# The beginning of feed-forward 1: 23 products of the tile of ones ahead of it, the third lower part ahead of the squares' sums, the fifth and sixth lower parts within the gating chain

## The chip, the cores and the metric

The kernel runs on one core of one Trainium2 chip. The metric is the device time of one launch in microseconds (us), the median of a few runs. The engines of the core that matter here are PE (matrix products), DVE (element-wise work), ACT (activations and copies), POOL (GpSimd) and SP, whose queue issues the loads of the weights. Each engine takes its instructions in the order in which they are written; engines wait for each other through semaphores.

## The reference

The program is a transformer block (a feed-forward network, a mixer of two attentions, a second feed-forward network) followed by a second, larger block, on 256 tokens of width 1024. The change touches only the beginning of the first feed-forward network:

```
def rms_norm(x, g):
    xf = x.astype(jnp.float32)
    y = xf * lax.rsqrt(jnp.mean(xf * xf, axis=-1, keepdims=True) + EPS)
    return (y * g.astype(jnp.float32)).astype(x.dtype)

def swiglu(x, w_gate, w_up, w_down):
    return (jax.nn.silu(x @ w_gate) * (x @ w_up)) @ w_down

f1 = swiglu(rms_norm(h, ffn1_pre_g[l]), ffn1_w_gate[l], ffn1_w_up[l], ffn1_w_down[l])
h = h + 0.5 * rms_norm(f1, ffn1_post_g[l])
```

The hidden width of this network is 2816, which is 22 chunks of 128 (FC = 22).

## The kernel before

The weights come as a stream of tiles of 128 by 1024 fp32 numbers (512 KB), in the order in which PE uses them, through a ring of six places (RING = 6). Feed-forward 1 uses 66 tiles: gate 0, up 0, gate 1, up 1, down 0, gate 2, up 2, down 1, and so on. Below, "tile 0" to "tile 5" are the first six of them. SP loads the place of a tile again when PE has counted up "tiles_used" for it.

Every product is made from two parts of each number. ACT copies a tile to a rounded upper part (`upper`), DVE subtracts that from the tile for the lower part (`lower`, an instruction of 128 by 1024; POOL does it for every third tile from tile 8 on), and PE makes three matmuls in place of one (`split_product`: upper by upper, upper by lower, lower by upper, lines 641 to 643). The input and the hidden chunks are split in the same way: `input_upper` and `lower_input` for the eight chunks of the input, `upper_hidden` and `lower_hidden` for a hidden chunk. One tile is 24 matmuls of 128x256.

The norm is applied late: the gate and up products are made from the input times its gain, without the inverse root. Meanwhile ACT squares the input in four pairs (`square_pair`), DVE adds the squares (`input_sums`, four additions), PE sums over the partitions (`add_squares`), ACT takes the root (`take_root`), DVE inverts it (`invert`), PE spreads the inverse over the partitions (`spread`), and ACT copies it to memory (`copy_inverse`). Only then can DVE scale the first gate product by it, ACT apply Silu, DVE multiply with the up product, ACT and DVE split the hidden chunk, and PE begin with `down(0, 4)`, the product of hidden chunk 0 with tile 4. This row of steps is called the gating chain below. Before it PE can do four tiles (`gate_up(0, 0)` is tiles 0 and 1, `gate_up(1, 2)` is tiles 2 and 3); `add_squares` and `spread` stand between products of the latter.

After the beginning a loop of nine turns runs over the rest of the hidden chunks. All engines' programs are written out by hand, so what the change moves is seen in the code itself. `ones` is a tile of 128 by 128 fp32 ones that DVE sets near the program's start; PE uses it for sums over partitions. `half_bank(MOD, 1)` is half a PSUM bank that nothing reads at this time.

Of the kernel before, what the change touches and what calls it, by code (L numbers as in the profile page):

```python
# [14 lines left out]
P = 128  # L15
# [7 lines left out]
RING = 6  # L23
# [317 lines left out]
def two_blocks(nc, dram):  # L341
    with ExitStack() as ctx:
# [85 lines left out]
        ones = view(MEM, "ones")  # L428
# [172 lines left out]
        def _(pe):  # L601
# [102 lines left out]
            def ffn(k):  # L704
                base = FC * k

                def gate_up(par, t, more=0, hid=None):
                    if hid is not None:
                        pe.wait_ge(S("hidden_ready"), hid)
                    for a in range(2):  # L710
                        w = split_tile(k, t + a, more)
                        if k == 0 and a == 1 and isinstance(more, int) and t == 2:
                            spread("ffn1_pre")
                        for c_ in range(DC):
                            if k == 0 and isinstance(more, int) and t == 0:
                                pe.wait_ge(S("input_split"), c_ + 1)
                            mm = split_product(half_bank(PJ[par], a), w, slice(c_ * P, (c_ + 1) * P),
                                               (u_hi[k][:, c_, :], u_lo[k][:, c_, :]),
                                               c_ == 0, c_ == DC - 1)
                            if k < 2 and a == 0 and c_ == 3 and isinstance(more, int) and t == 2:  # L720
                                square_sum_ready(f"ffn{k + 1}_pre", "square_sums", (1, 4)[k])
                                add_squares(f"ffn{k + 1}_pre", sq[:, 0, :], True, True)
                            if k == 1 and a == 0 and c_ == 5 and isinstance(more, int) and t == 2:
                                spread("ffn2_pre")
                        mm.then_inc(S("tiles_used"), 1)

                def gate_up_first():

                    for c_ in range(DC):
                        pe.wait_ge(S("input_split"), DC * k + c_ + 1)  # L730
                        for a in range(2):
                            mm = split_product(half_bank(PJ[0], a), split_tile(k, a), slice(c_ * P, (c_ + 1) * P),
                                               (u_hi[k][:, c_, :], u_lo[k][:, c_, :]), c_ == 0 and a == 0, c_ == DC - 1,
                                               skip_group_check=True)
                            if c_ == DC - 1:
                                mm.then_inc(S("tiles_used"), 1)

                def down(par, t, hid, first, last, more=0):
                    w = split_tile(k, t, more)
                    pe.wait_ge(S("hidden_split"), hid)  # L740
                    for n in range(DC):
                        mm = split_product(acc[n], w, slice(n * P, (n + 1) * P),
                                           (hidden_hi[k][:, par, :], hidden_lo[k][:, par, :]),
                                           first and n % 2 == 0, last, skip_group_check=True)
                        if last and n in (1, 3, 5):
                            mm.then_inc(S("down_pairs"), 1)
                    mm.then_inc(S("tiles_used"), 1)

                if k:
                    gate_up_first()  # L750
                else:
                    gate_up(0, 0)
                if k == 1:
                    pe.wait_ge(S("post_scaled"), 16)
                if k == 2:
                    pe.wait_ge(S("added"), 8)
                gate_up(1, 2)
                if k == 1:
                    pe.wait_ge(S("post_scaled"), 16)
                if k == 2:  # L760
                    pe.wait_ge(S("added"), 8)

                down(0, 4, base + 1, True, False)
                gate_up(0, 5, hid=base + 1)
                down(1, 7, base + 2, False, False)
                gate_up(1, 8, hid=base + 2)
                with pe.Fori(1, FC // 2 - 2) as i:
                    down(0, 4, i * 2 + (base + 1), False, False, i)
                    gate_up(0, 5, i, i * 2 + (base + 1))
                    down(1, 7, i * 2 + (base + 2), False, False, i)  # L770
                    gate_up(1, 8, i, i * 2 + (base + 2))
                down(0, 3 * FC - 8, base + FC - 3, False, False)
                gate_up(0, 3 * FC - 7, hid=base + FC - 3)
                gate_up(1, 3 * FC - 5, hid=base + FC - 2)
                down(1, 3 * FC - 3, base + FC - 2, False, False)
                down(0, 3 * FC - 2, base + FC - 1, False, False)
                down(1, 3 * FC - 1, base + FC, False, True)
# [24 lines left out]
                    mm.then_inc(S("tiles_used"), 1)  # L802


            pe.wait_ge(S("ones_ready"), 1)
            pe.wait_ge(S("ident_loaded"), 16)
            ffn(0)
            pe.wait_ge(S("tables_loaded"), 48)
# [653 lines left out]
        def _(act):  # L1462
# [72 lines left out]
            def feed_forward(k, gate, beside=lambda i: None, tail=lambda par: None):  # L1535
# [8 lines left out]
                for par in range(2):  # L1544
                    gate(par, par, k > 0, 0)
                    upper_hidden(k, par, FC * k + par)
                    upper(k, 6 + 3 * par)
                    upper(k, 7 + 3 * par)
                    upper(k, 8 + 3 * par)
# [70 lines left out]
            for i in range(4):  # L1620
# [2 lines left out]
                input_upper(0, 2 * i + 1, "ffn1_pre")  # L1623
                if i == 0:
                    uppers(0, 0, 1)
            uppers(0, 1, 2)
            for i in range(4):
                square_pair(i, h[:, 2 * i:2 * i + 2, :])
            uppers(0, 2, RING)
            take_root("ffn1_pre", D)  # L1630
            act.preload_act_table(ACT.Silu)
            act.wait_ge(S("vectors_loaded"), 16)
            act.activation(cond, vec[:, VEC["cond"]:VEC["cond"] + 16], ACT.Silu).then_inc(S("cond_ready"), 1)
            copy_inverse("ffn1_pre", inv)

            def tail_1(par):
                if par:
# [483 lines left out]
        def _(dve):  # L2121
# [97 lines left out]
            def feed_forward(k, product, beside=lambda i, par: None):  # L2219
# [11 lines left out]
                for par in range(2):  # L2231
                    product(par, par, 0)
                    lower_hidden(k, par, FC * k + par)
                    if k == 1 and par == 0:
                        lower(1, 5)
                    lower(k, 6 + 3 * par)
                    lower(k, 7 + 3 * par)
                def turn(i, beside):
# [18 lines left out]
            def ffn(k, beside=lambda i, par: None):  # L2257
                def multiply(par, f, more):
# [5 lines left out]
                    if k or not isinstance(f, int) or f > 1:  # L2264
                        dve.wait_ge(S("hidden_ready"), f + (FC * k - 1))
                    dve.tensor_tensor(silu[:, par, :], half_bank(PJ[par], 0), inv, ALU.mult)\
                       .then_inc(S("gates_scaled"), 1)
                    if k == 1 and isinstance(f, int) and f == 0:
                        lower(1, 4)
                    dve.wait_ge(S("silus"), f + (FC * k + 1))  # L2270
                    dve.tensor_tensor(hidden[:, par, :], silu[:, par, :], half_bank(PJ[par], 1), ALU.mult)\
                       .then_inc(S("hidden_ready"), 1)
# [47 lines left out]
            for n in range(DC):  # L2320
                lower_input(0, n, "ffn1_pre")
                if n == 1:
                    lower(0, 0)
            link(dve.tensor_scalar(half_gain, vec[:, 0:48], 0.5, None, ALU.mult))
            lower(0, 1)
            input_sums("ffn1_pre", sq)
            for j in range(2, RING):
                lower(0, j)
            invert("ffn1_pre")
            dve.wait_ge(S("vectors_loaded"), 16)  # L2330
            dve.wait_ge(S("cond_ready"), 1)
            ffn(0)
# [842 lines left out]
```

## Time and profile before

| what | number |
|---|---|
| runs of the kernel | 1203.77, 1205.46, 1205.49 us |
| median | 1205.46 us |
| span of the profiled execution | 1206.9 us |
| PE busy in it | 1178.4 us (98%) |
| DVE, ACT, POOL busy in it | 816.0, 637.3, 527.1 us |

The profiled execution is one of its own and not one of the three runs; its span is 1.4 us over their median. PE's busy time counts matmuls from issue to a modelled end, so it says that PE has few long gaps, not that it works at its peak. In the rows of the trace, a time is counted from the start of the span, "x4" is the number of instructions that a row joins, and a bracket tells how long the engine was idle and whose end released it.

### The profile page before, as it was taken

To read this page: it belongs to the slowest core of one execution; us is meant where nothing else is said; L and a number is where in the kernel's file an instruction comes from. 1 tells how busy PE (TensorE), PEld (TensorE's weight loads), DVE (VectorE), ACT (ScalarE), POOL (GpSimd) and SP (SyncE) were. 2 spreads that over 40 slices of the span, in tenths; PEclk is the share of its full clock that TensorE was granted. 3 is DMA by queue.
4 is the path that set the end of the run, shared out by engine and by line. 5 is a ranking of instruction groups with operands and counts; after the bars stand their busy time and mean duration, and the time that the engine had idled before them with its cause. 6 is when DMAs were issued, how large, how long until landed. Compare 5 with 4: busy or idle time off the path is not lost.

```text
span 1206.9 us, 24404 instructions
## 1 busy us (share of the span) xinstructions
PE 1178.4 (98%) x9128; PEld 1111.1 (92%) x9128; DVE 816.0 (68%) x1121; ACT 637.3 (53%) x1018; POOL 527.1 (44%) x285
## 2 busy tenths in 40 slices
PE   6999999999999999999999999999999999999998
PEld 6999999987889899999999879987877999999998
DVE  7788875856865577777654852688836596655555
ACT  6444446525762555454546546468517635655553
POOL 0343436732465533343436645458530483232331
PEclk9999998999999999999989999999999999999999
DMA  6888884543334467878614333233323254666663
GB/s 221 277 278 294 283 280 130 190 140 123 105 108 137 157 210 259 292 274 292 188 52 158 123 99 129 88 106 105 105 70 106 88 175 140 208 185 188 188 189 121
DMA packets 58100, 207.10 MB, mean 172 GB/s; under 512 B 6576, under 2 KB 8240, under 8 KB 57776
## 3 DMA queue, kind: packets, MB, share of 16 engines
q1 hardware_dynamic: 49824, 177.23, 45.2%
q0 software_dynamic: 6912, 25.17, 5.7%
q10 hardware_dynamic: 1296, 3.74, 0.9%
q8 instruction: 49, 0.80, 0.3%
q14 instruction: 19, 0.16, 0.1%
HBM read 205.07 MB, written 1.05 MB: 171 GB/s over the span
## 4 chain that ended last, share of the span: by engine, by line
PE 82%; DVE 8%; issue 3%; ACT 3%; POOL 2%; DMA 1%; DVEq 0%; SPq 0%; POOLq 0%; ACTq 0%
PE psum L641 23%; PE psum L642 23%; PE psum L643 22%; POOL own_parts L2944 2%; PE psum L789 1%; PE psum L1017 1%; PE psum L942 1%; PE psum L652 1%; PE psum L654 1%; PE psum L653 1%; PE psum L666 1%; PE psum L1346 1%; POOL high L3039 1%; DVE u_parts L2882 1%; PE psum L700 1%
## 5 line engine op out<-in xcount | busy, mean ns | idle before, releaser
L641 PE MATMUL psum<-parts 128*128 128x256 f32 x1584 | 441.0, 278 | 14.0 <-DVE parts L2197 10.4
L642 PE MATMUL psum<-parts 128*128 128x256 f32 x1584 | 445.7, 281 | 0.0
L643 PE MATMUL psum<-parts 128*128 128x256 f32 x1584 | 441.6, 279 | 0.0
L641 PEld LDWEIGHTS psum<-parts 128*128 128x128 f32 x1584 | 299.5, 189 | 14.9 <-issue 11.0
L2952 POOL TENSOR_TENSOR parts<-low,parts 128x1024 fp32r<-128x1024 f32 x60 | 151.0, 2517 | 367.4 <-ACT parts L1520 367.4
L643 PEld LDWEIGHTS psum<-parts 128*128 128x128 f32 x1584 | 299.7, 189 | 0.0
L642 PEld LDWEIGHTS psum<-parts 128*128 128x128 f32 x1584 | 299.7, 189 | 0.0
L1520 ACT ACTIVATE parts<-low 128x1024 fp32r<-128x1024 f32 x198 | 207.4, 1056 | 163.1 <-DMA low<-stream 162.4
L2944 POOL TENSOR_TENSOR own_parts<-low,parts 128x1024 fp32r<-128x1024 f32 x75 | 184.9, 2479 | 151.5 <-ACT parts L1598 147.4
L2197 DVE TENSOR_TENSOR parts<-low,parts 128x1024 fp32r<-128x1024 f32 x138 | 163.6, 1219 | 23.6 <-ACT parts L1520 22.9
L642 PE MATMUL psum<-u_parts,parts 128*128 128x256 f32 (+1 forms) x560 | 164.7, 294 | 0.0
L643 PE MATMUL psum<-scratch_parts,own_parts 128*128 128x256 f32 (+1 forms) x496 | 149.3, 301 | 0.0
L2944 POOL TENSOR_TENSOR own_parts<-low,single_upper 128x1024 fp32r<-128x1024 f32 x35 | 87.1, 2494 | 81.3 <-ACT single_upper L1598 77.5
L642 PEld LDWEIGHTS psum<-u_parts,parts 128*128 128x128 f32 x560 | 107.9, 193 | 2.5 <-issue 0.5
L643 PE MATMUL psum<-late_parts,own_parts 128*128 128x256 f32 x360 | 101.0, 280 | 0.0
L643 PEld LDWEIGHTS psum<-scratch_parts,own_parts 128*128 128x128 f32 x496 | 95.7, 193 | 3.7
L641 PE MATMUL psum<-late_parts,parts 128*128 128x256 f32 x320 | 92.5, 289 | 1.1 <-POOL own_parts L2944 1.1
L1598 ACT ACTIVATE parts<-low 128x1024 fp32r<-128x1024 f32 x75 | 78.4, 1051 | 16.2 <-DMA low<-stream 16.1
L642 PE MATMUL psum<-u_parts,single_upper 128*128 128x256 f32 (+1 forms) x280 | 82.8, 296 | 0.0
L641 PE MATMUL psum<-scratch_parts,single_upper 128*128 128x256 f32 (+1 forms) x256 | 79.9, 312 | 2.4 <-POOL own_parts L2944 1.7
L2203 DVE TENSOR_TENSOR parts<-low,parts 128x256 fp32r<-128x256 f32 x66 | 58.1, 880 | 32.3 <-ACT parts L1526 32.3
L2228 DVE SCALAR_TENSOR_TENSOR high<-high,low 128x1024 f32<-128x1024 f32 x64 | 79.0, 1273 | 0.0
(384 smaller groups left out, 2091.1 us busy)
## 6 DMA issues: line engine op xcount, KB each, us to landing
low<-stream SPq DMA_DIRECT2D x334, 512.0 KB, 3.6
high<-conditioning POOLq DMA_DIRECT2D x48, 512.0 KB, 5.0
high<-wuq ACTq DMA_DIRECT2D x1, 1152.0 KB, 5.1
low<-x SPq DMA_DIRECT2D x4, 256.0 KB, 6.3
high<-ctx ACTq DMA_DIRECT2D x1, 1024.0 KB, 6.4
out<-low SPq DMA_DIRECT2D x8, 128.0 KB, 1.8
low<-cst ACTq DMA_DIRECT2D x1, 850.5 KB, 4.8
low<-vec ACTq DMA_DIRECT2D x1, 157.5 KB, 6.3
```

Source lines behind the costliest of these rows:

```text
L641: pe.matmul(out, w_hi[:, cols_], x_hi, start=start, stop=False, **kw)
L642: pe.matmul(out, w_hi[:, cols_], x_lo, start=False, stop=False, **kw)
L643: return pe.matmul(out, w_lo[:, cols_], x_hi, start=False, stop=stop, **kw)
L652: pe.matmul(out, hi(k, n), w_hi[:, cols_], start=k == 0, stop=False)
L653: pe.matmul(out, hi(k, n), w_lo[:, cols_], start=False, stop=False)
L1520: act.activation(ring_hi[:, j % RING, :], ring[:, t % RING, :], ACT.Copy)\
L1598: act.activation(weight_place(t), ring[:, t % RING, :], ACT.Copy)\
L2197: dve.tensor_tensor(ring_lo[k][:, j % RING, :], ring[:, t % RING, :], ring_hi[:, j % RING, :], ALU.subtract).then_inc(S("lower_ready"), 1)
L2203: dve.tensor_tensor(hidden_lo[k][:, par, :], hidden[:, par, :], hidden_hi[k][:, par, :], ALU.subtract).then_inc(S("hidden_split"), 1)
L2228: dve.scalar_tensor_tensor(out=acc_, in0=cond_places[g], scalar=small[:, bass.ds(i * 2 + who, 1)], in1=acc_, op0=ALU.mult, op1=ALU.add).th ...
L2944: pool.tensor_tensor(tile_lo[:, t % RING, :], ring[:, t % RING, :], weight_place(t), ALU.subtract).then_inc(S("weights_split"), 1)
L2952: pool.tensor_tensor(ring_lo[k][:, j % RING, :], ring[:, t % RING, :], ring_hi[:, j % RING, :], ALU.subtract).then_inc(S("lower_ready_2"), 1)
```

## The change

On PE, the first instructions become 12 products of `ones` by `ones` (fp32, 128 columns) into a half bank that nothing reads, then a wait for the first quarter of the input, then 11 more. In the second half of tile 2's products the sum of squares moves from behind the fourth chunk to behind the second, and the spread of the inverse moves from ahead of tile 3 to behind the seventh chunk of tile 2. On ACT, the upper part of tile 2 comes ahead of the squares, tile 3's stays ahead of the root, tile 4's goes behind the copy of the inverse and tile 5's behind the first hidden chunk's upper part. On DVE, the lower part of tile 2 comes ahead of the sums of squares, tile 3's behind them, tile 4's in between the scaling of the first gate product and its multiplication, tile 5's behind the first hidden chunk's lower part; the small scaling of the gains (`half_gain`) moves from ahead of tile 1's lower part to behind the inverse.

```
@@ PE, gate_up
-                        if k == 0 and a == 1 and isinstance(more, int) and t == 2:
-                            spread("ffn1_pre")
...
-                            if k < 2 and a == 0 and c_ == 3 and isinstance(more, int) and t == 2:
+                            if k < 2 and a == 0 and c_ == (1, 3)[k] and isinstance(more, int) and t == 2:
                                 square_sum_ready(f"ffn{k + 1}_pre", "square_sums", (1, 4)[k])
                                 add_squares(f"ffn{k + 1}_pre", sq[:, 0, :], True, True)
-                            if k == 1 and a == 0 and c_ == 5 and isinstance(more, int) and t == 2:
-                                spread("ffn2_pre")
+                            if k < 2 and a == 0 and c_ == (6, 5)[k] and isinstance(more, int) and t == 2:
+                                spread(f"ffn{k + 1}_pre")
@@ PE, beginning
+            def keep_busy(count):
+
+                for _ in range(count):
+                    pe.matmul(half_bank(MOD, 1)[:, 0:P], ones, ones, start=True, stop=True, skip_group_check=True)
+
             pe.wait_ge(S("ones_ready"), 1)
+            keep_busy(12)
+            pe.wait_ge(S("x0_loaded"), 16)
+            keep_busy(11)
             pe.wait_ge(S("ident_loaded"), 16)
             ffn(0)
@@ ACT, feed_forward
                     upper_hidden(k, par, FC * k + par)
+                    if k == 0 and par == 0:
+                        upper(0, 5)
                     upper(k, 6 + 3 * par)
@@ ACT, beginning
-            uppers(0, 1, 2)
+            uppers(0, 1, 3)
             for i in range(4):
                 square_pair(i, h[:, 2 * i:2 * i + 2, :])
-            uppers(0, 2, RING)
+            uppers(0, 3, 4)
             take_root("ffn1_pre", D)
...
             copy_inverse("ffn1_pre", inv)
+            upper(0, 4)
@@ DVE, feed_forward and multiply
-                    if k == 1 and par == 0:
-                        lower(1, 5)
+                    if k < 2 and par == 0:
+                        lower(k, 5)
...
-                    if k == 1 and isinstance(f, int) and f == 0:
-                        lower(1, 4)
+                    if k < 2 and isinstance(f, int) and f == 0:
+                        lower(k, 4)
@@ DVE, beginning
+            lower(0, 1)
+            lower(0, 2)
+            input_sums("ffn1_pre", sq)
+            lower(0, 3)
+            invert("ffn1_pre")
             link(dve.tensor_scalar(half_gain, vec[:, 0:48], 0.5, None, ALU.mult))
-            lower(0, 1)
-            input_sums("ffn1_pre", sq)
-            for j in range(2, RING):
-                lower(0, j)
-            invert("ffn1_pre")
```

DVE's order from the last input chunks on, before (L2197 is the lower part of a tile, L2155 and L2156 are the sums of squares, L2135 the inverse, L2266 the scaling of the gate product, L2271 the multiplication, L2203 the lower part of the hidden chunk):

```order
L2209 SCALAR_TENSOR_TENSOR parts<-low,parts 128x256 x6
L2324 TENSOR_SCALAR high<-low 128x48
L2197 TENSOR_TENSOR parts<-low,parts 128x1024
L2155 TENSOR_TENSOR low<-low 128x512 x3
L2156 TENSOR_TENSOR low<-low 128x256
L2197 TENSOR_TENSOR parts<-low,parts 128x1024 x4
L2135 RECIPROCAL high<-high 128x2
L2137 SCALAR_TENSOR_TENSOR high<-high 128x2
L2266 TENSOR_TENSOR low<-psum,low 128x256
L2271 TENSOR_TENSOR low<-low,psum 128x256
L2203 TENSOR_TENSOR parts<-low,parts 128x256
```

And in the changed kernel (the same instructions stand nine lines further on, L2206 for L2197, L2338 for L2324):

```order
L2206 TENSOR_TENSOR parts<-low,parts 128x1024 x2
L2164 TENSOR_TENSOR low<-low 128x512 x3
L2165 TENSOR_TENSOR low<-low 128x256
L2206 TENSOR_TENSOR parts<-low,parts 128x1024
L2144 RECIPROCAL high<-high 128x2
L2146 SCALAR_TENSOR_TENSOR high<-high 128x2
L2338 TENSOR_SCALAR high<-low 128x48
L2275 TENSOR_TENSOR low<-psum,low 128x256
L2206 TENSOR_TENSOR parts<-low,parts 128x1024
L2280 TENSOR_TENSOR low<-low,psum 128x256
L2212 TENSOR_TENSOR parts<-low,parts 128x256
L2206 TENSOR_TENSOR parts<-low,parts 128x1024 x3
```

Of the four lower parts that stood between the sums and the inverse one is left there; one went ahead of the sums, one stands now between the scaling and the multiplication, and one stands behind the hidden chunk's lower part.

ACT's order from the last input chunks on, before (L1520 is the upper part of a tile, L1472 a pair of squares, L1480 the root, L1633 the Silu of the condition vector, L1503 the copy of the inverse, L1569 the Silu of the gate, L1526 the upper part of the hidden chunk):

```order
L1507 ACTIVATE parts<-low 128x256 x6
L1520 ACTIVATE parts<-low 128x1024
L1472 ACTIVATE low<-low 128x512 x4
L1520 ACTIVATE parts<-low 128x1024 x4
L1480 ACTIVATE high<-psum,low 128x2
L1631 ACT_TABLE_LOAD
L1633 ACTIVATE low<-low 128x16
L1503 ACTIVATE low<-psum 128x256
L1569 ACTIVATE low<-low 128x256
L1526 ACTIVATE parts<-low 128x256
L1520 ACTIVATE parts<-low 128x1024 x3
```

And in the changed kernel (L1526 is now the upper part of a tile, L1577 the Silu, L1532 the upper part of the hidden chunk):

```order
L1526 ACTIVATE parts<-low 128x1024 x2
L1478 ACTIVATE low<-low 128x512 x4
L1526 ACTIVATE parts<-low 128x1024
L1486 ACTIVATE high<-psum,low 128x2
L1639 ACT_TABLE_LOAD
L1641 ACTIVATE low<-low 128x16
L1509 ACTIVATE low<-psum 128x256
L1526 ACTIVATE parts<-low 128x1024
L1577 ACTIVATE low<-low 128x256
L1532 ACTIVATE parts<-low 128x256
L1526 ACTIVATE parts<-low 128x1024 x4
```

One upper part stands ahead of the squares, one stays behind them, and one has come between the copy of the inverse and the Silu of the gate.

## Rows read from the trace of the kernel before

**Rows 1.** The page's part 4: shares of the chain that ended last.
```profile
PE 82%; DVE 8%; issue 3%; ACT 3%; POOL 2%; DMA 1%; DVEq 0%; SPq 0%; POOLq 0%; ACTq 0%
```

**Rows 2.** Timeline of PE in the beginning: start, duration (us), engine, line, operation.
```profile
10.38 0.55 PE L641 MATMUL psum<-parts 128*128 128x256 f32 x1 [10.38 <-DVE parts L2197]
...
15.22 0.41 PE L642 MATMUL psum<-parts 128*128 128x256 f32 x1
...
18.40 0.28 PE L641 MATMUL psum<-parts 128*128 128x256 f32 x1
...
19.79 0.50 PE L666 MATMUL psum<-low 128*128 128x1 f32 x4
...
21.63 0.61 PE L700 MATMUL psum<-low,high 128*128 128x128 f32 x4
...
24.75 0.28 PE L643 MATMUL psum<-parts 128*128 128x256 f32 x1
25.18 0.36 PE L641 MATMUL psum<-parts 128*128 128x256 f32 x1
```

**Rows 3.** Timeline of DVE in the beginning.
```profile
1.14 0.17 DVE L2317 MEMSET low<- 128x128 f32 x1
...
8.90 1.23 DVE L2197 TENSOR_TENSOR parts<-low,parts 128x1024 fp32r<-128x1024 f32 x1 [0.39 <-ACT parts L1520]
10.04 2.46 DVE L2209 SCALAR_TENSOR_TENSOR parts<-low,parts 128x256 fp32r<-128x256 f32 x6
...
12.63 1.23 DVE L2197 TENSOR_TENSOR parts<-low,parts 128x1024 fp32r<-128x1024 f32 x1
13.78 2.13 DVE L2155 TENSOR_TENSOR low<-low 128x512 f32<-128x512 f32 x3
15.95 0.43 DVE L2156 TENSOR_TENSOR low<-low 128x256 f32<-128x256 f32 x1
...
20.83 0.16 DVE L2135 RECIPROCAL high<-high 128x2 f32<-128x2 f32 x1
...
22.79 0.42 DVE L2266 TENSOR_TENSOR low<-psum,low 128x256 f32<-128x256 f32 x1 [1.74 <-ACT low L1503]
23.70 0.42 DVE L2271 TENSOR_TENSOR low<-low,psum 128x256 f32<-128x256 f32 x1 [0.48 <-ACT low L1569]
24.61 0.43 DVE L2203 TENSOR_TENSOR parts<-low,parts 128x256 fp32r<-128x256 f32 x1 [0.49 <-ACT parts L1526]
...
29.64 0.82 DVE L2203 TENSOR_TENSOR parts<-low,parts 128x256 fp32r<-128x256 f32 x1 [0.48 <-ACT parts L1526]
```

**Rows 4.** Timeline of ACT in the beginning.
```profile
7.02 0.91 ACT L1507 ACTIVATE parts<-low 128x256 fp32r<-128x256 f32 x2 [3.43 <-DMA low<-x]
...
12.12 2.17 ACT L1472 ACTIVATE low<-low 128x512 f32<-128x512 f32 x4
14.20 3.88 ACT L1520 ACTIVATE parts<-low 128x1024 fp32r<-128x1024 f32 x4
20.39 0.26 ACT L1480 ACTIVATE high<-psum,low 128x2 f32<-128x2 f32 x1 [2.31 <-PE psum L666]
...
21.96 0.22 ACT L1633 ACTIVATE low<-low 128x16 f32<-128x16 f32 x1
22.28 0.38 ACT L1503 ACTIVATE low<-psum 128x256 f32<-128x256 f32 x1
23.25 0.42 ACT L1569 ACTIVATE low<-low 128x256 f32<-128x256 f32 x1 [0.59 <-DVE low L2266]
```

**Rows 5.** Loads of tiles 1 and 2 (line 583): issue, and time until the data had landed.
```profile
L583 SPq DMA_DIRECT2D low<-stream x2: 432/438/443, 3.4 to 3.9; - x2
DMA to landing us min/median/max: 7.3/7.7/8.1
```

**Rows 6.** Busy time by engine in two stretches; the last columns: granted clock, DMA share, GB/s.
```profile
45.00:65.00 20.00, 20.00 (x175) 20.00 (x174) 17.05 (x20) 9.95 (x14) 10.27 (x7) 1.00 0.84 293
418.50:425.20 6.70, 5.10 (x24) 5.10 (x25) 6.07 (x14) 4.82 (x11) 6.18 (x8) 0.50 0.00 0
```

## Prediction

> **What bounds the kernel now.** I read the chain that ended last first: PE carries 82% of it [rows 1]. Then PE's timeline of the beginning, to see how far the change reaches: PE starts at 10.38 us, when tile 0's lower part is ready, and reaches the first product of tile 4 (`down(0, 4)`) at 25.18 [rows 2]. After that, in a stretch of the loop, it has 175 matmuls in 20 us and is busy for all 20.00 [rows 6]. So every microsecond by which `down(0, 4)` starts earlier should arrive at the end, as long as the loop's loads and lower parts follow; they are released by PE's own counts and move with it.
>
> In those 14.8 us PE does four tiles. Two things cost more than the matmuls do.
>
> First, the clock. Tiles 0 and 1 (48 matmuls) take 10.38 to 18.40, 8.02 us; the next 12 take 18.40 to 19.79, 0.116 us each [rows 2]. At that pace 48 would take 5.56, so 2.46 us are lost. A matmul at 15.22 still lasts 0.41, one at 18.40 lasts 0.28 [rows 2]: the first is TensorE's level of 1.2 GHz, the second that of 2.4. About 5 us of products went ahead of the rise.
>
> Second, the gating chain. The last product of tile 3 starts at 24.75 and that of `down(0, 4)` at 25.18, 0.43 later in place of 0.116 [rows 2]. The hidden chunk's lower part runs 24.61 to 25.04 [rows 3], so PE waited 0.3 us for it. PE and the chain are thus nearly level: speeding up PE alone gives nothing unless the chain's start, which hangs on PE (`add_squares`, `spread`), gets earlier too.
>
> **The change part by part.**
>
> *Products of ones.* `ones` is set at 1.31 [rows 3]. The pair of spreads, two fp32 products of 128 columns, and the 23 matmuls after it take 21.63 to 24.75, 3.12 us; less 23 × 0.116 leaves 0.45, so 0.23 for one [rows 2], and I estimate 0.46 at the lower level. The first 12 would fill 1.3 to at most 6.8. The input's first quarter is there by 7.02 [rows 4], so the other 11 start about 7.05. Before, some 5 us of products were enough for the rise; 5 us after 1.3 is 6.3, so I expect the 11 to be at the higher level, 2.5 us, done by 9.6, ahead of 10.38. They delay nothing and tile 0 begins at 2.4 GHz. The 128 by 256 products of tile 0 are fed by the input's lower parts: the last six take 10.04 to 12.50, 0.41 each [rows 3], against 3 × 0.116 = 0.35 on PE, so tile 0 ends near 13.2 and starts no earlier than before.
>
> *Tiles 1 and 2.* Without `half_gain` in front, tile 1's lower part starts at about 12.45 in place of 12.63 and ends 13.68. From a lower part's end to PE took 8.90 + 1.23 = 10.13 to 10.38, 0.25 [rows 2, 3]. Tile 1 starts at 13.93. Tile 2's data were issued by 3.9 and landed 8.1 later, 12.0 [rows 5], just when ACT becomes free at 12.12 [rows 4]; upper part 12.12 to 13.16. Lower part on DVE 13.60 (from one such instruction to the next is 13.78 − 12.63 = 1.15 [rows 3]) to 14.83. PE never waits on it: tile 1 and two chunks of tile 2 are 30 matmuls, 3.48, so 17.41.
>
> *Sums.* The squares start one upper part later on ACT: about 13.1 to 15.3, where it was 12.12 to 14.29 [rows 4]. DVE is free at 14.75; the sums take 13.78 to 16.38, 2.60 [rows 3], now to 17.35, where they were long ready before. `add_squares` starts at 17.55 (latency 0.2) in place of 19.79: 2.24 earlier. PE stands 0.14 for it.
>
> *Spread.* `add_squares` and 12 matmuls took 19.79 to 21.63, 1.84 [rows 2], so add_squares 0.45. Five chunks of tile 2 follow, 1.74: spread at 19.74 in place of 21.63. The root comes 0.60 after the sum (20.39 [rows 4]), 18.15, and the inverse 0.44 later (20.83 [rows 3]), behind tile 3's lower part, which DVE holds until 18.5: 18.7 at the latest. It is ready. From root to the end of the condition's Silu ACT takes 20.39 to 22.18, 1.79 [rows 4], so free at 19.94. The copy follows the spread's start by 0.65 (21.63 to 22.28 [rows 2, 4]): 20.39, in place of 22.28. So far 1.89 us are won.
>
> *Inside the gating chain.* The scaling starts 0.51 behind the copy [rows 3, 4]: 20.90. But tile 4's upper part now stands on ACT behind the copy: four such take 3.88 [rows 4], about 1.0 each, so 20.77 to 21.8. Tile 4's lower part on DVE waits for it and holds DVE until the multiplication can start, 1.15 later: 22.98. Before, the multiplication stood 0.91 behind the scaling (22.79 to 23.70 [rows 3]); now it is 2.08. The move gives back 1.17 of the 1.89. The Silu also queues behind the upper part, at 21.8 in place of 0.46 behind the scaling, but ends by 22.25, hidden beside the lower part. From multiplication to lower part 0.91, to PE 0.57 (24.61 to 25.18 [rows 2, 3]): `down(0, 4)` at 24.46. PE is done with tile 3 at 19.74 + 0.45 + 27 × 0.116 = 23.32, so it stands for about 1.1 us: that is the new wait.
>
> *Tile 5 and on.* ACT does tile 5's upper part 23.8 to 24.8, DVE tiles 5, 6 and 7 24.8 to 28.3. PE needs tile 5 at 24.46 + 2.78 = 27.24, hidden by `down(0, 4)`. The second hidden chunk then starts at 28.3, and with 0.91 + 0.91 + 0.82 its lower part ends at 30.9, where it was 29.64 + 0.82 = 30.46 [rows 3]. PE wants it after three tiles, 24.46 + 8.34 = 32.8: 1.9 us of cover. Gone, it would cost the difference directly.
>
> *Sum.* 25.18 − 24.46 = 0.72 us earlier. The profiled execution has a span of 1206.9, so 1206.2. Its span is 1.4 over the median of the runs; I take 0.72 off that as well: 1205.46 − 0.72 = 1204.7. One part in 1700: less than the 0.2% (2.4 us) that a measurement of this kernel tells from no change.
>
> *Bounds.* If tile 4's lower part cost the chain nothing, the multiplication would follow the Silu at 22.25 and `down(0, 4)` would start at 23.73, and PE itself allows 23.63: at most 1.5 us gained. The other end is the clock, below.
>
> The cold term itself differs between executions. The Trainium skill ("TensorE: Matmul & The Clock Gate", What's actually happening) says that the same kernel shows a different number of slow matmuls from run to run, since the gate's window doesn't start with the kernel. By that rule the 2.46 us in other executions of before are some less or more. The three runs agree with such a scatter, 1.7 us from lowest to highest, but don't show its cause.
>
> **The rivals.**
>
> *1. The chain hides better (up to 1.5 to 2 us gained).* For it: the chain from 17.55 on is made of latencies, and the upper part on ACT could overlap more. Against: both instructions stand in order on their engines, and neither can pass. Span 1205.0, runs 1203.9 to 1203.4.
>
> *2. The clock doesn't stay up to 10.38 (slower).* PE idles about 0.3 to 1 us between the bursts and again before 10.38. In 418.5 to 425.2 the granted clock is 0.50 while PE is busy 5.10 of 6.70 us [rows 6], so the clock does fall in this kernel when PE has had pauses. Here the pauses are smaller than the work between them. Then tiles 0 and 1 run as before, tile 2 starts at 18.40, `add_squares` at 19.10, spread 21.29, copy 21.94, multiplication 24.5, `down(0, 4)` 26.0: 0.8 us slower, 1206.3 for the runs.
>
> *3. The burst itself stands in the way (slower).* If the level rises after 8.7 rather than by 7, the 11 products end after 10.38: at the lower level throughout they take 5.06, until 12.1. Tile 0 then starts 1.7 late and, with the rise where it was, tile 2 0.8 late: 1.7 us slower in all, up to 2.5 if the rise is late too: 1207.2 to 1208.0. Against: 7 us of nearly unbroken products from 1.3 on, where 5 were enough.
>
> *4. Nothing arrives.* The 0.7 us are lost where a load or POOL is the limit in the loop. Against: PE busy 20.00 of 20 us [rows 6]. 1205.5.
>
> The Trainium skill (same page, "Why this matters for your kernels") advises keeping TensorE busy first to get past the slow level. By that alone, taking the whole cold term out, the sum would be 2.46 us and the runs 1203.0. The trace speaks against the full sum: PE starts tile 1 only when its lower part is there, and the chain ends later than PE.
>
> **How the numbers follow.** My forecast 0.60; rival 1 0.20; rival 2 0.07; rival 3 0.06; rival 4 0.07. The likeliest is 1204.7. With a scatter of the runs' median of about 1 us on each side, the forecast and rivals 1 and 4 span 1202.8 to 1206.4, which takes in rival 2 as well; only rival 3 and the tails are left out. Faster by over 0.2% needs below 1203.05: a third of rival 1 and one in six of the forecast, 0.17. Slower by over 0.2% needs above 1207.9: half of rival 3 and a tail, 0.05. Within: 0.78.
>
> **What the profile after would show.** The products of ones: from about 1.4, a second burst from 7.05, the last ones about 0.23 apart, done before 10. The first matmul of tile 0 at 10.4 with a duration of 0.28, not 0.41 to 0.55. Tile 1 from 13.9. Squares' sum on PE at 17.5, spread at 19.7. On DVE a lower part of 1.23 between L2275 and L2280, 2.1 us from one to the other. PE idle about 1.1 us ahead of `down(0, 4)`, which starts at 24.5, released by L2212. PE's loop without waits. I would be wrong if `down(0, 4)` stands at 23.6 or at 26, or if it stands at 24.5 and the span doesn't follow; if the first matmul is at 12, rival 3 holds.

## The result and the profile after

The changed kernel takes 1214.01 us in the median of 22 runs (1209.83 to 1218.19), the kernel before 1206.78 in 22 (1203.77 to 1217.05). The ratio estimated from the runs is 1.0046, with a 95% interval of 1.003 to 1.0061 (the quotient of the two medians is 1.0060): 0.46% slower, where 0.06% faster was forecast and a range that ended at 1206.4. The head of the kernel (what comes before tile 4) did what was predicted. The loss is in the loop behind it, which the prediction took for granted.

Timeline of PE in the changed kernel's beginning (the profiled execution has a span of 1212.8 us):

```profile
1.36 4.51 PE L806 MATMUL psum<-low 128*128 128x128 f32 x24 [1.36 <-DVE low L2326]
6.76 2.72 PE L806 MATMUL psum<-low 128*128 128x128 f32 x22 [0.88 <-DMA low<-x]
10.04 0.35 PE L641 MATMUL psum<-parts 128*128 128x256 f32 x1 [0.56 <-issue]
...
17.16 0.60 PE L666 MATMUL psum<-low 128*128 128x1 f32 x4
...
19.46 0.61 PE L700 MATMUL psum<-low,high 128*128 128x128 f32 x4
...
24.08 0.36 PE L641 MATMUL psum<-parts 128*128 128x256 f32 x1 [0.88 <-DVE parts L2212]
```

The products of ones are done ahead of tile 0, tile 0 runs with durations of 0.28 to 0.35 us (the 2.4 GHz level, by the durations) where [rows 2] had 0.41 and 0.55, and the wait that I named stands ahead of `down(0, 4)`: 0.88 us. The input landed 0.2 us earlier in this execution than in the one of before, so 24.08 is 0.2 better than a like start would give.

Timeline of DVE: the new lower part inside the gating chain, against [rows 3].

```profile
20.62 0.42 DVE L2275 TENSOR_TENSOR low<-psum,low 128x256 f32<-128x256 f32 x1 [2.14 <-ACT low L1509]
21.47 1.22 DVE L2206 TENSOR_TENSOR parts<-low,parts 128x1024 fp32r<-128x1024 f32 x1 [0.43 <-ACT parts L1526]
22.61 0.41 DVE L2280 TENSOR_TENSOR low<-low,psum 128x256 f32<-128x256 f32 x1
23.50 0.42 DVE L2212 TENSOR_TENSOR parts<-low,parts 128x256 fp32r<-128x256 f32 x1 [0.48 <-ACT parts L1532]
```

From scaling to multiplication 1.99 us; I had 2.08.

Then the loop. Busy time by engine in three stretches of the changed kernel (columns as in [rows 6]):

```profile
45.00:65.00 20.00, 18.27 (x154) 17.67 (x153) 16.35 (x14) 8.54 (x11) 9.60 (x6) 1.00 0.74 245
60.00:80.00 20.00, 19.59 (x167) 19.38 (x168) 18.06 (x18) 9.93 (x13) 9.70 (x6) 1.00 0.71 235
80.00:100.00 20.00, 19.59 (x169) 19.39 (x168) 18.06 (x17) 7.59 (x10) 12.10 (x6) 1.00 0.80 284
```

PE has 154 matmuls in 45 to 65 us where it had 175, and 163 to 169 in each 20 us from 60 to 180. At a granted clock of 1.00 this is waiting. PE's waits from 25 to 198 us (engine and line, what it waited for, us in total, times, longest) follow; the kernel before has none there. They count from a matmul's modelled end, 0.16 us past the start of the next at full pace, so they add up to less than the loss.

```profile
PE psum L641 <- DVE parts L2212: 3.5, 9, 0.4
PE psum L641 <- DVE parts L2206: 1.1, 1, 1.1
```

The sum of squares behind feed-forward 1 (L677 on PE) gives the account. First the kernel before, then the changed one:

```profile
197.22 0.50 PE L677 MATMUL psum<-high,low 128*128 128x1 f32 x4
```

```profile
204.20 0.50 PE L677 MATMUL psum<-high,low 128*128 128x1 f32 x4
```

6.98 us later, from a start that was 1.10 earlier: the loop and its end cost 8.1 us. The rest of the kernel took 1212.8 − 204.2 = 1008.6 against 1206.9 − 197.2 = 1009.7. In these two profiles the whole loss is in feed-forward 1.

**What a slow turn is.** DVE in the changed kernel from 68 to 92 us (L2237 conditioning additions, L2206 the turn's pair of lower parts), then POOL's lower parts (L2961) and loads (L2984) in the same time:

```profile
68.75 3.67 DVE L2237 SCALAR_TENSOR_TENSOR high<-high,low 128x1024 f32<-128x1024 f32 x3
72.34 2.35 DVE L2206 TENSOR_TENSOR parts<-low,parts 128x1024 fp32r<-128x1024 f32 x2
...
79.55 4.56 DVE L2206 TENSOR_TENSOR parts<-low,parts 128x1024 fp32r<-128x1024 f32 x2
84.03 0.41 DVE L2275 TENSOR_TENSOR low<-psum,low 128x256 f32<-128x256 f32 x1
```

```profile
72.14 4.82 POOL L2961 TENSOR_TENSOR parts<-low,parts 128x1024 fp32r<-128x1024 f32 x1 [6.02 <-ACT parts L1526]
76.90 1.10 POOL L2984 DMA_DIRECT2D high<-conditioning  x2
79.72 3.31 POOL L2961 TENSOR_TENSOR parts<-low,parts 128x1024 fp32r<-128x1024 f32 x1 [1.72 <-ACT parts L1526]
```

Two lower parts of DVE take 2.35 us alone and, when POOL's lies across them, 2.35 or 4.56; POOL's takes 2.4 alone and 3.3 to 4.8 across DVE's. At 72.14 both together end at 76.96, 4.82 later, about 2.35 + 2.4: the two engines take turns, they don't share. In the pair at 79.55 the turns can be seen singly: DVE's first instruction takes 1.21 us, its second, from 80.69, takes 3.42 while POOL's ends at 83.03. The Trainium skill ("GPSIMD Engine Reference", Specifications) says that POOL's way to SBUF is shared with VectorE and contends with its instructions of two SBUF inputs, which these are; the trace agrees. A turn of the loop has two pairs of DVE, and one of them is slow. With that the turn is 96.98 − 79.55 = 17.43 us long, where PE's 144 matmuls need 16.7 (144 × 0.1157).

**What tips it.** ACT's upper part of tile 14 starts at 44.16 in the kernel before, at 45.80 in the changed one, although PE freed its place 1.1 us earlier. First ACT (tiles 11 and 14) and POOL (part and two loads) of the kernel before:

```profile
36.20 1.06 ACT L1520 ACTIVATE parts<-low 128x1024 fp32r<-128x1024 f32 x1 [3.28 <-DMA low<-stream]
...
44.16 1.06 ACT L1520 ACTIVATE parts<-low 128x1024 fp32r<-128x1024 f32 x1 [2.27 <-DMA low<-stream]
```

```profile
30.12 0.70 POOL L2959 DMA_DIRECT2D high<-conditioning  x1
37.35 2.40 POOL L2952 TENSOR_TENSOR parts<-low,parts 128x1024 fp32r<-128x1024 f32 x1 [6.53 <-ACT parts L1520]
39.70 1.10 POOL L2959 DMA_DIRECT2D high<-conditioning  x2
```

And of the changed kernel:

```profile
33.62 1.06 ACT L1526 ACTIVATE parts<-low 128x1024 fp32r<-128x1024 f32 x1 [1.80 <-DMA low<-stream]
...
45.80 1.06 ACT L1526 ACTIVATE parts<-low 128x1024 fp32r<-128x1024 f32 x1 [5.39 <-DMA low<-stream]
```

```profile
30.16 0.70 POOL L2968 DMA_DIRECT2D high<-conditioning  x1
34.77 2.39 POOL L2961 TENSOR_TENSOR parts<-low,parts 128x1024 fp32r<-128x1024 f32 x1 [3.92 <-ACT parts L1526]
37.12 1.10 POOL L2968 DMA_DIRECT2D high<-conditioning  x2
```

Read step by step: POOL's first load goes out at the same time in both (30.1), but PE frees tile 11's place 1.1 us earlier. SP's request for tile 11, in the kernel before and in the changed one:

```profile
31.15 0.33 SPq L588 DMA_DIRECT2D low<-stream  x1
```

```profile
30.05 0.33 SPq L588 DMA_DIRECT2D low<-stream  x1
```

So tile 11 is asked for ahead of that load, by 0.1 us, and not 1.0 us behind it, and ACT can begin with it 2.6 us earlier. POOL's next lower part and the two loads behind it move up by the same 2.6 us, to 37.1, ahead of tile 14's request (38.4) and no longer behind it (39.5). Issues and median time to landing from 39.0 to 41.3 us in the kernel before, and from 36.5 to 40 in the changed one:

```profile
high<-conditioning POOLq DMA_DIRECT2D x2, 512.0 KB, 6.0
low<-stream SPq DMA_DIRECT2D x1, 512.0 KB, 4.6
```

```profile
high<-conditioning POOLq DMA_DIRECT2D x2, 512.0 KB, 6.8
low<-stream SPq DMA_DIRECT2D x1, 512.0 KB, 7.3
```

ACT waits 5.39 us for that tile with the Silu of the next gate queued behind it, and DVE and PE are held. From then on the tiles are mostly there when ACT comes to them, so POOL's lower part starts together with DVE's pair.

### The profile page after: what moved, and what is told of

Same layout as the page of the kernel before. It is cut to its first block, busy times and chain, and to the rows that moved or that the text cites. A ratio compares the mean times of both kernels' runs of the same rounds, so it can differ in the third digit from the quotient of the medians.

```text
span 1212.8 us, 24493 instructions
## 1 busy us (share of the span) xinstructions
PE 1183.4 (98%) x9174; PEld 1112.4 (92%) x9174; DVE 835.5 (69%) x1121; ACT 634.9 (52%) x1018; POOL 545.0 (45%) x285
## 4 chain that ended last, share of the span: by engine, by line
PE 69%; DVE 15%; issue 5%; ACT 4%; POOL 4%; DMA 2%; DVEq 0%; SPq 0%; POOLq 0%; ACTq 0%
PE psum L641 19%; PE psum L642 19%; PE psum L643 18%; DVE parts L2206 4%; POOL own_parts L2953 2%; DMA low<-stream 2%; POOL high L3048 1%; PE psum L787 1%; DVE high L2237 1%; PE psum L1023 1%; PE psum L948 1%; PE psum L652 1%; PE psum L654 1%; PE psum L653 1%; PE psum L666 1%
## 5 line engine op out<-in xcount | busy, mean ns | idle before, releaser
L2961 POOL TENSOR_TENSOR parts<-low,parts 128x1024 fp32r<-128x1024 f32 x60 | 169.6, 2826 | 356.6 <-ACT parts L1526 356.6
L1526 ACT ACTIVATE parts<-low 128x1024 fp32r<-128x1024 f32 x198 | 205.9, 1054 | 124.4 <-DMA low<-stream 123.4
L2206 DVE TENSOR_TENSOR parts<-low,parts 128x1024 fp32r<-128x1024 f32 x138 | 181.5, 1346 | 20.2 <-ACT parts L1526 19.3
L2237 DVE SCALAR_TENSOR_TENSOR high<-high,low 128x1024 f32<-128x1024 f32 x64 | 79.0, 1274 | 0.0
L2212 DVE TENSOR_TENSOR parts<-low,parts 128x256 fp32r<-128x256 f32 x66 | 54.0, 818 | 32.3 <-ACT parts L1532 32.3
```

The costliest lines, as they stand in the source:

```text
L1526: act.activation(ring_hi[:, j % RING, :], ring[:, t % RING, :], ACT.Copy)\
L2206: dve.tensor_tensor(ring_lo[k][:, j % RING, :], ring[:, t % RING, :], ring_hi[:, j % RING, :], ALU.subtract).then_inc(S("lower_ready"), 1)
L2212: dve.tensor_tensor(hidden_lo[k][:, par, :], hidden[:, par, :], hidden_hi[k][:, par, :], ALU.subtract).then_inc(S("hidden_split"), 1)
L2237: dve.scalar_tensor_tensor(out=acc_, in0=cond_places[g], scalar=small[:, bass.ds(i * 2 + who, 1)], in1=acc_, op0=ALU.mult, op1=ALU.add).th ...
L2961: pool.tensor_tensor(ring_lo[k][:, j % RING, :], ring[:, t % RING, :], ring_hi[:, j % RING, :], ALU.subtract).then_inc(S("lower_ready_2"), 1)
```

## Experiments

The ratios below are to runs of the kernel before taken beside the experiments: medians 1209.08 (e1 to e4), 1209.02 (e5 to e8) and 1208.95 (e9 to e12), some 2.2 us above the 1206.78 of the result. So a difference from the changed kernel's 1214.01 is told too small by about that much; the ratios are the safer measure. "Before" and "changed" are the two kernels of the result. Each experiment has one profile, which need not be a typical execution of it.

**Parts alone, and PE's phase.** The first kernel is before plus the 23 products (and the wait between them); the second is the changed kernel without them; the third and fourth are the changed kernel with:

```
# e3_pe_later
+                if k == 0:
+                    pe.wait_ge(S("hidden_split"), 1)
+                    stay_awake(9, u_hi[0])
                 down(0, 4, base + 1, True, False)
# e4_cond_behind_tile14 (POOL)
+                        if par:
+                            pool.wait_ge(S("slot2_loaded"), 48)
                         for g in ((0,), (1, 2))[par]:
                             first_tile(g)
```

> The kernel before with only the 23 products of ones in front; every lower and upper part and both norm steps stand where they stood. Theory A (the loop of feed-forward 1 is tipped by when PE starts it: PE early, so tiles are freed and gates are ready early, and the conditioning vectors' first pair of loads gets in ahead of tile 14, whose upper part then holds ACT): the first product of tile 4 comes 1 to 2 us earlier than in the kernel before (25.2), and if the shift of the load pattern is enough the loop shows PE waits on the hidden chunks and the time is 3 to 7 us over that of the kernel before. Theory B (the new order of lower and upper parts on DVE and ACT is what costs, whatever the clock): no waits in the loop, lower parts at 1.15 us, the time 1 to 2 us under the kernel before. Theory C (scatter between runs, no cause in the kernel): as before.

1215.92 us (6 runs), ratio 1.0054 (1.0036 to 1.0071). `down(0, 4)` at 24.74. The products of ones alone, with no order changed, are enough for the loss. But the way there was another: ACT and POOL are earlier too (POOL's first load at 29.69, tile 11's request at 30.72), so the order and the distance of these two are those of the kernel before, and tile 14 still landed ahead (ACT at 43.32). The tile that came late was tile 17 (ACT waits 4.06 us, until 54.23), and the slow pairs begin at 60.38. Its profile is of the slowest of the six runs.

> The changed kernel without the 23 products of ones. Tiles 0 and 1 run at the lower level of the clock again; I expect the first product of tile 4 at 25 to 26 us, no earlier than before. Theory A: with PE as late as before, the conditioning loads fall behind tile 14 again, no waits in the loop, 0 to 1 us over the kernel before. Theory B: the loop waits as in the changed kernel, 5 to 8 us over the kernel before.

1214.70 us (6 runs), ratio 1.0059 (1.0043 to 1.0075). Theory A in this form fell: `down(0, 4)` starts at 25.62, later than before, and the loop is slow all the same. PE's absolute time isn't what counts. In this kernel the second hidden chunk's lower part is at 31.22, in place of 29.64 [rows 3], so DVE, ACT and POOL are later still than PE: tile 11 is asked for at 31.60 and POOL's first load goes out at 31.71, again 0.1 us behind it, as in the changed kernel.

> The changed kernel, with 9 more products of 256 columns (1.05 us) into the unread half bank between the wait for hidden chunk 0's parts and the first product of tile 4. DVE and ACT keep the changed order; only PE's phase goes back to that of the kernel before (first product of tile 4 near 25.1). Theory A: the loop is fast again, no waits on the hidden chunks, tile 14 lands ahead of the second and third conditioning load, and the time is that of the kernel before within 1 us, so 5 to 7 us under the changed kernel although PE does more work. Theory B: 1 us slower than the changed kernel.

1209.96 us (12 runs), ratio 0.9997 (0.9978 to 1.0016). More work on PE, 4 us less time than the changed kernel. The order at 30 us is back: POOL's first load at 29.99, tile 11's request at 30.88. Its profile, of one of the faster runs (1206.75), has no PE waits from 25 to 198 us, `down(0, 4)` at 25.00, L677 at 197.18, and the pairs of lower parts at 2.35.

> The changed kernel, in which POOL issues the first loads of conditioning vectors 1 and 2 only when tile 14 has landed. Nothing else moves. Theory A, in its form that the collision of these two loads with tile 14 is the trigger: tile 14 lands near 43 us, ACT's wait of 5.4 us for it shrinks to about 2, the loop has no PE waits, and the time is 1 us under the kernel before. If the collision is only a companion and PE's early phase by itself keeps the loop slow, or the two loads now hit tiles 15 and 16 instead, the waits stay and so do the 5 to 7 us. Theory B: as the changed kernel.

1214.68 us (7 runs), ratio 1.0052 (1.003 to 1.0073). Tile 14 did come early (ACT 42.00, a wait of 1.70), and a later turn tipped instead: the first slow pair is at 59.4. Keeping one collision away isn't enough.

**What keeps the loop slow.** The changed kernel without the loop's 21 conditioning loads (DVE adds old data); POOL made to wait for DVE's pair, in the changed kernel and in the kernel before; DVE's pair ahead of the conditioning additions:

```
# e5_no_cond_loads (POOL; DVE waits for the first loads alone)
-                            for g in ((0,), (1, 2))[par]:
+                            for g in ((0,), (1, 2))[par] if k else ():
# e6_pool_behind_pair, e7_before_pool_behind_pair (POOL)
+                            if k == 0:
+                                pool.wait_ge(S("lower_ready"), i * 4 + (12 + 2 * par))
                             lower(k, 14 + 3 * par, i)
# ... the same ahead of the two lower parts before the loop, with 8 + 2 * par;
# none ahead of the four behind the loop
# e8_pair_ahead_of_cond (DVE)
-                        beside(i, par)
                         lower(k, 12 + 3 * par, i)
                         lower(k, 13 + 3 * par, i)
+                        beside(i, par)
```

> The changed kernel without the 21 conditioning loads of feed-forward 1's loop (the first three stay, DVE's additions run as often on old data, so the modulation is not the reference's). Theory A1 (two transfers that meet are what holds a tile back, and that tips the loop): every run is fast, no PE waits in the loop, the slow pairs of lower parts (4.55 us for two) are gone, the runs lie within 3 us of each other at 1 us or more under the fastest runs of the kernel before, 1203. Theory A2 (the early start of PE against DVE and ACT is enough, loads are only a companion): the waits of about 0.4 us a turn stay, 1211 to 1216.

1213.56 us (8 runs), ratio 1.0044 (1.0023 to 1.0065). The first three loads had stayed, so tile 14 came late as before (ACT 44.80, a wait of 4.23); after that no conditioning load was left in the loop, and the slow pair came back every turn up to 164 us. Once tipped, the loop stays slow with no load to push it.

> The changed kernel; POOL waits, ahead of each of its lower parts in feed-forward 1, until DVE has done its two lower parts of the same turn. In the changed kernel's profile they run at once, 4.55 us for DVE's two in place of 2.35. Theory: this overlap is what keeps the loop slow once a late tile has tipped it; then DVE is 2.2 us a turn less behind, PE's waits vanish a turn or so after a tip, and the time is 1204 to 1207, narrower than the kernel before. If the overlap is only a symptom, the waits and the 1211 to 1216 us stay.

1208.31 us (12 runs), ratio 0.9993 (0.9976 to 1.0011). Lower parts on DVE from 30 to 185 us (count, busy us, mean ns), in the changed kernel and here:

```profile
L2206 DVE TENSOR_TENSOR parts<-low,parts 128x1024 fp32r<-128x1024 f32 x36 | 60.1, 1706 | 0.5 <-ACT parts L1526 0.2
```

```profile
L2206 DVE TENSOR_TENSOR parts<-low,parts 128x1024 fp32r<-128x1024 f32 x38 | 44.9, 1215 | 4.5 <-ACT parts L1526 4.3
```

Tile 14 was as late as in the changed kernel (ACT 45.02, a wait of 4.61): the trigger was there, and the loop recovered, with one wait of 0.2 us on PE in all. L677 at 196.86. So the overlap is what keeps the loop slow. The waits also move POOL's later loads, but e5 has shown that the loop stays slow without any. A wait added to POOL is worth 5 us here.

> The kernel before with the same waits of POOL. Its own runs scatter from 1204 to 1217, which I read as the turn in which the loop tips, each slow turn costing about 0.75 us. If the waits cure it, the median falls from about 1208 to about 1205 and the scatter to 3 us; about 1 us over the changed kernel with the same waits. If the scatter has another cause it stays.

1207.97 us (12 runs, 1204.04 to 1212.12), ratio 0.9993 (0.9976 to 1.0009). Not told from the kernel before. My reading of the scatter as the turn in which the loop tips isn't borne out. The one slow pair of its profile, at 159.74, is beside a lower part of POOL that the edit gave no wait.

> The changed kernel; DVE does its two lower parts of a turn ahead of the conditioning additions (three times 1.2 or two times 1.2 us) and not behind them. The pair is then ready earlier and mostly done before POOL's lower part starts. If what matters is that the pair and POOL's part don't run at once, the loop recovers as with POOL's waits: 1204 to 1208. If the conditioning loads set the pace, they are released later (their places are read later) and hit other tiles: 1208 to 1216.

1237.27 us (6 runs), ratio 1.0268 (1.0233 to 1.0303). Both branches missed. The pairs are at 2.36, but POOL issues each conditioning load behind a wait for DVE's additions, with its next lower part queued behind it: POOL waited 40.2 us on L2237 and PE 18.2 on hidden chunks.

**The trigger, both ways.** POOL's first load ahead of its first lower part, without and with the waits of e6; a single conditioning load (vector 0's first) in all of feed-forward 1 (e10); and the kernel before with one wait more:

```
# e9_cond0_first, e11_both (POOL)
+                if k == 0:
+                    first_tile(0)
...
-                        for g in ((0,), (1, 2))[par]:
+                        for g in ((), (1, 2))[par]:
# e12_before_cond0_later (POOL)
+                        if par == 0:
+                            pool.wait_ge(S("tiles_used"), 6)
                         for g in ((0,), (1, 2))[par]:
                             first_tile(g)
```

> The changed kernel; POOL issues the first conditioning load (vector 0) ahead of its lower part of tile 8, at about 27.5 us in place of 30.2. In the kernel before that load landed at 35.0, ahead of tile 11 (36.3); in the changed kernel PE frees tile 11's place 1.1 us earlier, tile 11 lands first (33.6), POOL gets on to its next lower part 2.6 us earlier, the loads of vectors 1 and 2 go out at 37.1 in place of 39.7, and tile 14 lands behind them (45.7) and not ahead. Theory T (this order of loads tips the loop): with vector 0 first again tile 11 lands near 35.5, tile 14 ahead of vectors 1 and 2, and the time is that of the kernel before or 1 us less. Rival P (PE ahead of DVE and ACT by itself leaves too little slack, whatever the loads): waits and 1211 to 1216 as in the changed kernel.

1212.05 us (12 runs), ratio 1.0032 (1.0009 to 1.0055). The edit did something else than I meant: nothing held POOL back until 27.5, so the load went out at 20.27 and was long done, and tile 11 stayed early. Tile 14 was late again and the pair at 52.6 was slow (4.56), but in this profile the loop recovered in the next turn and L677 is at 198.44. The test that was meant is e12, from the other side.

> The changed kernel with only one conditioning load in feed-forward 1 (vector 0, once); vectors 1 and 2 are never loaded there and DVE's additions for them read their own sums in place of the data, as long and as often as before (the modulation is not the reference's). Theory T: nothing is left that could put tile 14 or a later one back, so the loop is never tipped: all runs within 3 us, near 1203 to 1205, no slow pairs of lower parts. Rival P: the loop is slow all the same, 1211 to 1216.

1208.66 us (12 runs, 1202.93 to 1212.28), ratio 0.999 (0.9969 to 1.0011). No slow pair in its profile, no PE waits, L677 at 196.59. Rival P is out: PE's lead by itself doesn't slow the loop. The runs still scatter by 9 us, with nothing here to tip them.

> The changed kernel with both: vector 0's load ahead of POOL's first lower part, and POOL's lower parts behind DVE's pair of the same turn. Candidate for a version that beats the kernel before: the head's 1.1 us kept, no slow state. Theory T with the overlap as what sustains it: 1204 to 1207, 1 to 3 us under the kernel before. If the loads' order matters little once POOL waits: as with POOL's waits alone, 1208.

1207.78 us (12 runs), ratio 0.9994 (0.9972 to 1.0015). As e6; not told from the kernel before, so no version that beats it was found.

> The reverse test: the kernel before, in which POOL issues vector 0's first load only when PE has used tile 5 (30.7 us in place of 30.1), so that tile 11's load goes out first. PE, DVE and ACT are untouched. Theory T: tile 11 lands first (near 34.5), POOL is earlier by about 2 us with vectors 1 and 2, tile 14 lands behind them, and the loop tips as in the changed kernel: 1211 to 1216 with no change to the head at all. Rival P: as the kernel before, 1208.

1212.49 us (12 runs, 1204.85 to 1215.76), ratio 1.0033 (1.0012 to 1.0053). The head is that of the kernel before, untouched; one load goes out 0.5 us later, at 30.58, behind tile 11's request at 30.44. ACT (tiles 11 and 14), and PE's waits from 25 to 198 us:

```profile
34.19 1.06 ACT L1520 ACTIVATE parts<-low 128x1024 fp32r<-128x1024 f32 x1 [1.89 <-DMA low<-stream]
...
46.01 1.06 ACT L1520 ACTIVATE parts<-low 128x1024 fp32r<-128x1024 f32 x1 [5.17 <-DMA low<-stream]
```

```profile
PE psum L641 <- DVE parts L2203: 3.3, 9, 0.4
PE psum L641 <- DVE parts L2197: 1.0, 1, 1.0
```

The same signature as the changed kernel, wait for wait, and L677 at 204.38. In this profile the order of two requests at 30 us decides over 7 us. It is of one of the slowest runs (1215.71), and its head happens to be 0.7 us faster than in the profile of before (`down(0, 4)` at 24.46); by the medians the order is worth 3.5 us, so this profile can't stand for every execution.

## Why the prediction was wrong

*Products of ones, clock:* right. They ended before tile 0, and 2.46 us of slow products are gone. Each took a little less than I had, from one start to the next: 0.43 us at the lower level (0.46 predicted) and 0.22 at the higher (0.23). The rise came within the first burst, at 4.7 us, and the level held to tile 0 across the two pauses. The levels are read from these distances: the profile's clock column is 1.00 in these stretches of both kernels, also from 12 to 14 us of the kernel before, where a matmul came every 0.213 us. That the cold term differs between executions is borne out: with the head unchanged, PE has 23 slow steps in the profile of before, 18 in e7's and 17 in e12's, and `down(0, 4)` starts at 25.18, 24.76 and 24.46.

*Sums, spread, gating chain:* right in mechanism and near in size. `add_squares` 17.16 (17.55 predicted), spread 19.46 (19.74), `down(0, 4)` 24.08 (24.46), the wait on PE 0.88 (1.1). The head won 1.10 us, of which about 0.2 is the earlier input; 0.72 was the term.

*Second hidden chunk:* right. It ended at 30.5 (30.9 predicted) and PE didn't wait.

*The step that failed* stands in the first paragraph: every microsecond should arrive at the end "as long as the loop's loads and lower parts follow; they are released by PE's own counts and move with it". The tiles' loads are. The conditioning loads are released by POOL, behind ACT's upper parts and DVE's additions, and those didn't move: POOL's first lower part ended at 30.2 in both kernels. Rows for them were not read. The head moved PE by 1.1 us against POOL, which swapped two requests. Rival 4 ("nothing arrives") was the nearest, but it priced the loop at zero at worst and rested on PE busy for 20.00 of 20 us in [rows 6]. That row says that the loop had no wait, not how far it was from one. The missing term is 8.1 us: about 2.6 in three waits of PE between 49 and 63 us, behind the late tile 14, and then some 0.77 (17.43 − 16.66) in each of seven turns.

*The price of overlap* of DVE's and POOL's lower parts was also not in the sum. It could be read before: in [rows 3] the hidden chunk's lower part takes 0.43 at 24.61 and 0.82 at 29.64, where POOL was at work.

*The scatter of 1.7 us* that I took from three runs was far too small: 22 runs of the same kernel span 13 us. What causes it is open; neither the order of loads (e10) nor the overlap (e7) accounts for it. A part lies outside this loop: behind L677, where the edits of e1 and e3 change nothing, their profiles take 1013.9 and 1007.9 us. So of the 9.4 us between e1's profile and that of before, 5.2 are in feed-forward 1.

*What stays open.* The swap at 30 us tipped the changed kernel and e12, but it isn't the only way: e1 tipped without it and e4 in spite of an early tile 14, each seen in one profile. Which of the later collisions did it there was not tried. What the profiles have in common is this: up to 170 us ACT waits over 4 us for a tile, once, in each kernel whose loop went slow with such pairs (the changed one, e1, e2, e4, e5, e9, e12) and in e6 and e11, where POOL's waits let it recover; it never does in the kernel before, e3, e7 and e10. So the loop tips at a late tile, and the overlap holds it slow. Other tiles come late only behind 170 us, where the loop ends, in fast kernels too.

## What to carry to other kernels

A loop that a profile shows fully busy can still have a second way to run, in which the same work collides every turn; before a head is sped up, list each load or instruction in the loop that is released by another engine than the one that gets faster, and see which requests would change places. Where two engines take turns at one resource, as DVE and POOL did here in their two-input subtractions, an explicit wait that orders them can cost nothing (e7) and take the slow way out: e6 is 5 us faster than the changed kernel. And a gain of 1 us can't be shown where runs scatter by 9.

## What was not expected of the hardware

DVE's two lower parts and POOL's one took 4.56 to 4.82 us together, about the sum of each alone (2.35 and 2.4), and which of them stood still differed between the two halves of a turn: at 72.14 DVE kept its 2.35, at 79.55 it took 4.56. Two conditioning loads of 512 KB asked for 1.2 us ahead of a tile's raised its time to landing to 7.3 us; it was 4.6 with them asked for 0.2 us behind it, and 3.5 with none near (e4, e10).
